# Stick-breaking attention: queries or keys on the partitions, the running sum as triangle products or as scans

## The reference

```python
def block(args):
    qblk, qi = args
    z = jnp.einsum('bhqd,bhkd->bhqk', qblk, kh).astype(jnp.float32) * scale
    strict = kidx[None, :] < qi[:, None]
    log_beta = jax.nn.log_sigmoid(z)
    log_1mb = jnp.where(strict, jax.nn.log_sigmoid(-z), 0.0)
    between = lax.cumsum(log_1mb, axis=3, reverse=True) - log_1mb
    a = jnp.exp(jnp.where(strict, log_beta + between, -jnp.inf))
    return jnp.einsum('bhqk,bhkd->bhqd', a, vh)
```

## Time and profile before

| | us |
|---|---|
| median of three runs | 2451.89 (2450.37 to 2454.68) |
| profiled execution | 2442.98 |
| its span | 2441.2 |
| TensorE busy | 2342.7 (96%) |
| VectorE busy | 1131.7 (46%) |
| ScalarE busy | 852.2 (35%) |
| GpSimd busy | 541.6 (22%) |

### The profile page before, as it was taken

One profiled execution on the slowest core, in us unless ns is written; L12 is line 12 of the kernel. 1 busy time (PEld: TensorE's weight loads), 2 busy tenths in 40 slices (PEclk: granted clock), 3 DMA queues, 4 the chain that ended last, 5 costly groups with the idle time before them and its releaser, 6 DMA issues.

```text
span 2441.2 us, 34782 instructions
## 1 busy us (share of the span) xinstructions
PE 2342.7 (96%) x14548; PEld 1771.8 (73%) x14548; DVE 1131.7 (46%) x1498; ACT 852.2 (35%) x1468; POOL 541.6 (22%) x244
## 2 busy tenths in 40 slices
PE   7999999999999998999999999999999999999997
PEld 4777765555578775878888888888767677778875
DVE  6776745446566244352112122122434656477554
ACT  4444455556535222142022122022333522354321
POOL 2321212111120221321212222222222122213221
PEclk9999999999999998999999999999999999999999
DMA  3211101103023010111111111112221001100022
GB/s 135 72 46 50 52 26 35 52 26 121 27 79 129 26 35 10 51 37 50 52 43 52 43 52 43 52 43 70 83 75 44 18 27 43 37 27 12 4 105 78
DMA packets 37276, 126.03 MB, mean 52 GB/s; under 512 B 3856, under 2 KB 4368, under 8 KB 36752
## 3 DMA queue, kind: packets, MB, share of 16 engines
q1 hardware_dynamic: 30864, 103.30, 13.7%
q10 hardware_dynamic: 6272, 20.69, 2.2%
HBM read 114.53 MB, written 8.91 MB: 51 GB/s over the span
## 4 chain that ended last, share of the span: by engine, by line
PE 87%; DVE 7%; ACT 4%; issue 1%; DMA 0%; ACTq 0%; DVEq 0%
PE PS L186 22%; PE PS L188 21%; PE PS L187 21%; PE PS L902 2%; PE PS L1906 2%; PE PS L887 2%; PE PS L739 1%; PE PS L762 1%; PE PS L1144 1%; PE PS L914 1%; PE PS L1121 1%; PE PS L927 1%; PE PS L320 1%; PE PS L1527 1%; DVE arena L401 1%
## 5 line engine op out<-in xcount | busy, mean ns | idle before, releaser
L186 PE MATMUL PS<-u_r,w_hi 128*128 128x512 f32 x1280 | 520.4, 407 | 8.7 <-DVE arena_r L196 3.5
L188 PE MATMUL PS<-u_r,w_lo 128*128 128x512 f32 x1280 | 505.6, 395 | 0.0
L196 POOL TENSOR_TENSOR w_lo<-w_raw,w_hi 128x1024 fp32r<-128x1024 f32 x143 | 360.8, 2523 | 587.6 <-ACT w_hi L192 581.6
L187 PE MATMUL PS<-arena_r,w_hi 128*128 128x512 f32 (+1 forms) x1152 | 439.3, 381 | 0.0
L235 POOL TENSOR_TENSOR w_hi<-w_raw,const 128x1024 fp32r<-128x1024 f32 x77 | 151.1, 1962 | 1202.3 <-PE PS L186 1050.9
L186 PEld LDWEIGHTS PS<-u_r,w_hi 128*128 128x128 f32 x1280 | 240.6, 188 | 87.9 <-issue 16.0
L188 PEld LDWEIGHTS PS<-u_r,w_lo 128*128 128x128 f32 x1280 | 240.8, 188 | 57.0
L187 PEld LDWEIGHTS PS<-arena_r,w_hi 128*128 128x128 f32 x1152 | 217.0, 188 | 43.2 <-issue 0.7
L186 PE MATMUL PS<-h_r,w_hi 128*128 128x512 f32 x512 | 210.5, 411 | 4.3 <-DVE u_r L409 4.0
L188 PE MATMUL PS<-h_r,w_lo 128*128 128x512 f32 x512 | 202.9, 396 | 0.0
L187 PE MATMUL PS<-y_r,w_hi 128*128 128x512 f32 x512 | 201.0, 393 | 0.0
(11 more groups left out here) (395 smaller groups left out, 3547.9 us busy)
## 6 DMA issues: line engine op xcount, KB each, us to landing
w_raw<-in_w SPq DMA_DIRECT2D x174, 512.0 KB, 3.6
arena<-in_w SPq DMA_DIRECT2D x10, 512.0 KB, 5.2
h<-in_xT ACTq DMA_DIRECT2D x1, 4096.0 KB, 14.3
u<-parked_stream ACTq DMA_DIRECT2D x1, 4096.0 KB, 13.0
out<-arena SPq DMA_DIRECT2D x16, 256.0 KB, 2.0
parked_stream<-h ACTq DMA_DIRECT2D x6, 512.0 KB, 2.7
h<-in_xT SPq DMA_DIRECT2D x8, 256.0 KB, 7.4
h<-in_xT ACTq DMA_DIRECT2D x8, 256.0 KB, 9.2
```

Of the source, the lines that this page charges most:

```text
L186: first = pe.matmul(out, a[0], b[0], start=start, stop=False)
L187: pe.matmul(out, a[0], b[1], start=False, stop=False)
L188: return first, pe.matmul(out, a[1], b[0], start=False, stop=stop)
L196: return e.tensor_tensor(out, x, hi_part.bitcast(F), ALU.subtract)
```

## The change

Queries stand on the partitions and keys along the columns. An item is now one block of 128 queries against up to four key blocks, the nearest keys first; a unit still has 12 items and the same number of blocks. Their sizes in order are 1, 2, 3, 4, 1, 4, 2, 4, 3, 4, 4, 4.

- The running sum over keys is a scan along the columns, from right to left, on VectorE: one for each head, its two inputs max(z, 0) and the log, its start the sum left by the item before. The triangle products, the column totals, the decay, the 0/1 mask and the accumulation of the output on VectorE are gone.
- ScalarE writes max(z, 0) with a Relu from the score banks. VectorE then subtracts the sums from the scores.
- The weights need keys on the partitions for the value product: TensorE transposes the exponents block by block into bank 6, in one round (both heads, up to two blocks) or two (one head each), and ScalarE's Exp takes each round out.
- The value products accumulate in bank 7 over all key blocks of four query blocks; ScalarE copies them out twice a unit. They are one block pair of 128 columns at a time.
- The mask product is made with the scores.
- Chunks of q, k, v are made in two halves of 12 products (`part`), spread over the items. The "w" chunks stand one item later, the last one behind the last item.
- Transposes and weights run two items behind the scores, values three.
- Three constants (384 columns) are no longer loaded. One of the two weight tiles lies in `pos_f`, free at that time.

The core of the diff:

```diff
+        SB_PARTS = {j: {s: [(c, s % 2)] for s in range(12) for c in [("qkv"[s // 4], N_DA + j + 1, s // 2 % 2)]} for j in range(2)}
+        SB_PARTS[2] = {s: [(("qkv"[n // 4], UNITS - 1, n // 2 % 2), n % 2) for n in ns]
+                       for s, ns in enumerate(((0, 1), (2, 3), (4,), (5,), (6, 7), (8,), (9,), (10,), (11,)))}
...
-        SB_ITEMS = [(kb, half) for kb in range(4) for half in range(2)] + [(kb, 1) for kb in range(4, NT)]
+        SB_ITEMS = [(t, lo) for t in range(NT) for lo in (range(0, t + 1, 4))[::-1]]
...
+        def sb_scores(pe, g):
+            w, s = N_DA + g // SB_N, g % SB_N
+            t, lo, n, cols = sb_item(g)
+            if g >= 2:
+                pe.wait_ge(S("sb_e"), g - 1)
...
+                m = pe.matmul(bank(2 + 2 * (g % 2) + hd)[:, :cols], q[r, t * P:(t + 1) * P], k[r, lo * P:lo * P + cols],
+                              start=True, stop=not diag)
...
+        def sb_turn(pe, g, rd):
+            t, lo, n, cols = sb_item(g)
+            pe.wait_ge(S("sb_e"), g + 1)
+            if sb_turned(g, rd) > 1:
+                pe.wait_ge(S("sb_a"), sb_turned(g, rd) - 1)
...
+            for x, hd in enumerate(hds):
+                for b in range(n):
+                    m = pe.transpose(bank(6)[:, (x * n + b) * P:(x * n + b + 1) * P], Eb[:, g % 2, hd, b * P:(b + 1) * P], cst("ident"))
+            m.then_inc(S("sb_turned"), 1)
+
+        def sb_values(pe, g):
...
+            for b in range(n):
+                for hd in range(2):
+                    m = pe.matmul(PS[64 * hd:64 * hd + 64, 7 * HALF + t % 4 * P:7 * HALF + (t % 4 + 1) * P],
+                                  values_of(w)[1][:, lo + b, 64 * hd:64 * hd + 64], AT[g % 2][:, hd, b * P:(b + 1) * P],
+                                  start=first and b == 0, stop=last and b == n - 1)
+            m.then_inc(S("sb_av"), 1)
 
         def sb_pe(pe, g):
             if g < SB_ALL:
...
+                sb_scores(pe, g)
+            if g < 2:
+                da_values(pe, DA_N - 2 + g)
+            if 2 <= g < SB_ALL + 2:
+                sb_turn(pe, g - 2, 0)
+            if g < SB_ALL:
+                for c, part in sb_parts(*divmod(g, SB_N)):
+                    chunk_pe(pe, c, part)
+            elif g == SB_ALL:
+                chunk_pe(pe, CHUNK_ORDER[-1])
...
+            if 3 <= g < SB_ALL + 3:
+                sb_values(pe, g - 3)
+            if 2 <= g < SB_ALL + 2 and len(sb_rounds(g - 2)) > 1:
+                sb_turn(pe, g - 2, 1)
...
         def sb_act(act, g):
             if g < SB_ALL:
                 act.wait_ge(S("sb_z"), g + 1)
                 if g >= 2:
-                    act.wait_ge(S("sb_sp"), g - 1)
+                    act.wait_ge(S("sb_sums"), g - 1)
                 act.activation(sb_cols(ab, g), sb_z(g), ACT.Abs).then_inc(S("sb_abs"), 1)
+            if 2 <= g < SB_ALL + 2:
+                sb_weights(act, g - 2, 0)
+            if g < SB_ALL:
                 act.wait_ge(S("sb_abs"), g + 1)
                 act.activation(sb_cols(ab, g), sb_cols(ab, g), ACT.Exp, scale=-1.0).then_inc(S("sb_exp"), 1)
+                if g >= 2:
+                    act.wait_ge(S("sb_sums"), g)
+                    act.wait_ge(S("sb_e"), g - 1)
+                act.activation(sb_cols(sp, g), sb_z(g), ACT.Relu).then_inc(S("sb_relu"), 1)
                 act.wait_ge(S("sb_exp"), g + 1)
                 act.activation(sb_cols(ab, g), sb_cols(ab, g), ACT.Ln, bias=1.0).then_inc(S("sb_ln"), 1)
...
             if g < SB_ALL:
-                for c in sb_chunks(g // SB_N, g % SB_N):
+                for c in sb_chunks(*divmod(g, SB_N)):
                     chunk_act(act, c)
+            if 3 <= g < SB_ALL + 3:
+                sb_take_o(act, g - 3)
+            if 2 <= g < SB_ALL + 2 and len(sb_rounds(g - 2)) > 1:
+                sb_weights(act, g - 2, 1)
...
         def sb_dve(dve, g):
             if g < SB_ALL:
                 j, s = divmod(g, SB_N)
+                t, lo, n, cols = sb_item(g)
                 dve.wait_ge(S("sb_ln"), g + 1)
+                dve.wait_ge(S("sb_relu"), g + 1)
+                whole = lo + n == t + 1
+                for hd in range(2):
+                    sums = sp[:, g % 2, hd, :cols][:, ::-1]
+                    m = dve.tensor_tensor_scan(sums, sums, ab[:, g % 2, hd, :cols][:, ::-1],
+                                               0.0 if whole else sp[:, (g - 1) % 2, hd, 0:1], ALU.add, ALU.add)
+                m.then_inc(S("sb_sums"), 1)
+                dve.wait_ge(S("sb_sums"), g + 1)
                 if g >= 2:
...
+                    dve.wait_ge(S("sb_turned"), sb_turned(g - 2, len(sb_rounds(g - 2)) - 1))
+                dve.tensor_tensor(sb_cols(Eb, g), sb_z(g), sb_cols(sp, g), ALU.subtract).then_inc(S("sb_e"), 1)
```

More of the change, by code:

```diff
@@ L414, in in_, with chunk_product @@
             return lambda k, lo, hi: t[:, k, lo:hi]
-        def chunk_product(pe, g, b, x, h, width=T, ready=None, order=range(KC), free=None, inner=None, at=0):
+        def chunk_product(pe, g, b, x, h, width=T, ready=None, order=range(KC), free=None, inner=None, at=0, part=None):
             w = min(width, HALF)
             for k in order:
+                if part is not None and k // (KC // 2) != part:
+                    continue
                 if k == order[3] and inner is not None:
@@ L642, in chunk_pe @@
                 g = 3 * w + UNIT_PANEL[what]
-                if h == 0:
+                if h == 0 and part != 1:
                     panel_in(pe, g)
@@ L650, in ready @@
                         wait_split(pe, "mix", h)(k)
-                m = chunk_product(pe, g, b, u_mix, h, ready=ready, free=(h == 1) if w == 0 and what == "k" else None)
-            m.then_inc(S("proj_mm"), 1)
+                m = chunk_product(pe, g, b, u_mix, h, ready=ready, free=(h == 1) if w == 0 and what == "k" else None, part=part)
+            if part != 0:
+                m.then_inc(S("proj_mm"), 1)
         def chunk_act(act, c):
@@ L856, in sb_item, with sb_rounds @@
+        AT = [t.rearrange("p (h k) -> p h k", h=2) for t in (ar.take(T), pos_f)]
         def sb_item(g):
-            kb, half = SB_ITEMS[g % SB_N]
-            lo = max(kb * P, half * HALF)
-            return kb, lo, (half + 1) * HALF, kb // 4 == half
+            t, lo = SB_ITEMS[g % SB_N]
+            n = min(t + 1 - lo, 4)
+            return t, lo, n, n * P
         SB_ALL = (UNITS - N_DA) * SB_N
-        SB_CARRY = [g for g in range(SB_ALL) if sb_item(g)[0] > 0]
-        SB_DIAG = [g for g in range(SB_ALL) if sb_item(g)[3]]
+        def sb_rounds(g):
+            n = sb_item(g)[2]
+            return [(0, 1)] if n <= 2 else [(0,), (1,)]
@@ L866, in sb_z, with sb_turned @@
+        def sb_turned(g, rd):
+            return sum(len(sb_rounds(x)) for x in range(g)) + rd + 1
         def sb_z(g):
-            kb, lo, hi, diag = sb_item(g)
-            return bank(2 + 2 * (g % 2), 2).rearrange("p (h q) -> p h q", h=2)[:, :, :hi - lo]
+            return bank(2 + 2 * (g % 2), 2).rearrange("p (h k) -> p h k", h=2)[:, :, :sb_item(g)[3]]
         def sb_cols(t, g):
-            kb, lo, hi, diag = sb_item(g)
-            return t[:, g % 2, :, :hi - lo]
+            return t[:, g % 2, :, :sb_item(g)[3]]
@@ L2570, in _ @@
             dve.wait_ge(S("const_late"), 16)
[L2571 removed]
+            for g in range(SB_ALL + 1):
                 sb_dve(dve, g)
[L2573 to L2574 removed]
             y1_dve(dve, KC)
@@ L2791, in _ @@
                 da_act(act, g)
-            for g in range(SB_ALL + 1):
+            for g in range(SB_ALL + 3):
                 if g == SB_ALL - SB_N - 3:
@@ L2973, in _ @@
                 da_pe(pe, g)
-            for g in range(SB_ALL + 1):
+            for g in range(SB_ALL + 2):
                 sb_pe(pe, g)
```

198 lines of the change are left out of this document (74 added, 124 removed).

## The result

The changed kernel takes 2410.68 us (median, 2409.01 to 2415.41), the kernel before on the same chip 2451.3: a ratio of 0.9835, interval 0.9818 to 0.9852, so 40.6 us less, where 27 less had been forecast. A second run of both on another occasion gave 2410.77 and 2449.58, ratio 0.984 (0.9826 to 0.9853).

What follows compares the result with a forecast made beforehand. TensorE's work was taken to bound the stick-breaking stage. Its units summed to 308.5 us against 340.1 (-32); charging 4 for VectorE beside GpSimd and 1 for the clock left -27 from the median 2451.89: 2425 us, range 2401 to 2446.

Steps and rivals of the forecast that it cites:

- TensorE's terms: Stick-breaking stage: triangle products -66, column totals -26, values +8, transposes +32; net -52 us, the most that can be won.
- the longer of both engines at each item: Stage: neither TensorE nor ScalarE runs a step ahead, so each step takes the longer; middle unit 66, with additions 73.
- ScalarE's price: Stage: Relu 39 and other terms priced by instruction durations; ScalarE rises by about 30 us to 230.
- The fourth unit: Last unit of the stage: longer ones 64, with additions 70, then a 7.5 tail; 77.5 us against 81.6.
- The 4 us charged for VectorE's place: Stage: scans and GpSimd operations lock each other out in SBUF; 4 us charged, with 0 and 57 as ends.
- the additions of 3, 1 and 3: Middle unit: 3 us for ways between engines, 1 for instruction gaps, 3 that the same arithmetic missed before.
- the rival of the doubled scan: Stage: a scan pair takes 4.8 us, breaking the cover in 24 four-block items; +21, 2473; within a 0.08 chance.
- my own case: Whole kernel: 15 to 42 us faster, 2410 to 2437 us, chance 0.60.
- the case of TensorE alone: Stage: ScalarE's longer steps overlap shorter neighbours, only TensorE counts; -45 to -52, 2400 to 2407; chance 0.12.
- Doubled hand-overs: Stage: exchanges between engines cost about twice as much; only -7 to -13, 2439 to 2445; chance 0.14.
- VectorE as the bound: Stage: the scan pair waits out GpSimd (+28, 2480) or runs longer backwards; slower; chance 0.08.
- table loads: Stage: Relu needs two loads of 1.283 us for each of 48 items on ScalarE; +33, 2485; chance 0.01.

Runs made afterwards that it cites:

- Experiment 1: Changed kernel with each ScalarE instruction of a step made to wait for the one before it; 2434.92 us, 0.9961 of the kernel before.
- experiment 2: Two edits of the changed kernel: max(z, 0) left out, the scan taking the log twice, 0.9804; the maximum on VectorE instead of ScalarE, 0.9843.
- the second trace: Another trace of the unaltered changed kernel; its stage takes 305.9 us, where the first trace has 301.9.
- experiment 5: Changed kernel, seam of third and fourth unit: unneeded products added 0.9854; new values' transposes apart 0.9841; both 0.9831; transposes apart and seam rearranged 0.9814, with added products 0.9817.
- experiment 3: Changed kernel with the scan replaced by a plain addition of the same inputs, the running sum left out; 0.9798 of the kernel before.
- experiment 4: Changed kernel with whole q, k, v chunks at their old items, 0.9924; kernel before with only the halves spread over the items, 0.9988.

## Why the prediction was right in direction and too small

- **TensorE's terms.** Net 52 us to win at most; its busy time in the stage fell by 44.7. In the middle unit, at a granted clock of 1.00 on both sides, it fell by 12.9 us (80.15 to 67.23), a quarter of 52. The transposes' group has 288 records with 49.3 us busy, less 0.17 for each of 80 rounds 36, where 32 was priced. The price of the middle unit, 63, plus the 3 us that the same arithmetic had missed before, is 66; TensorE is busy 67.2 there. This held.
- **The step that failed: the longer of both engines at each item.** Over TensorE's 66 the prediction put 7 us for ScalarE's longer steps, gaps and hand-overs in the middle unit; 3.2 us of idle time were there (70.4 less 67.2), of it 1.4 at item 0 (the evacuation) and 1.25 at item 4 (the scan beside GpSimd), so next to nothing was left for ScalarE's longer steps. The mis-sized term is ScalarE's price: durations, 230 us, where the starts follow 0.10 to 0.12 us closer, 211 us. Experiment 1 gives ScalarE that price back, and somewhat more, and the middle unit goes to 78.7; experiment 2 takes Relu away, and the steps said to be bound by ScalarE don't move. By units: 72.2, 70.4 and 76.9 against 76, 73 and 82, in all 11.5 us better (8.5 by the second trace).
- **The fourth unit.** 77.5 predicted, 82.4 measured. VectorE's crowd at the seam had been priced as two longer ScalarE steps (7.0, 6.8) in the third unit and nothing in the fourth, whose items 0 and 1 took 7.4 and 7.3 us, though item 0 has no piece of the projection. Of the 7.3 some 1.6 are the clock's (experiment 5), for which the prediction had put 1 us and said that TensorE had slack; it had slack at the seam and none behind it. The 4 us charged for VectorE's place are there in size: 3.2 us in front of item 5 of three units, the rest at this seam.
- **Sum.** Stage 308.5 + 5 charged, against 301.9: 11.6 us less; 27 became 38.2 in the stage. By the second trace, 305.9, it is 7.6 less and 34.2. The sum has a slip: the additions of 3, 1 and 3 are 7, as in the middle unit, but by the figures given the third and fourth unit got 6; with 7 the stage would be 310.5 and the gain 25. In the rival of the doubled scan 4.8 less 2.8 is 2.0, not 2.2, so 2468 and not 2473. Of the signs named, TensorE's busy time (281), the scans at 1.2 and the waits of the transposes came; ScalarE near 230 did not, and the unit least improved is the fourth, not the third.
- **The scans.** 1.2 us for 512 columns, backwards and in place, is right (the median of all 96 is 1.199); the mean of the 512-column ones is 1.447, because GpSimd's operations hold some up to 3.0. The mechanism was right, and it is small on the path: 9 to 10 us for the whole scan length (experiment 3), seam included.
- **The rivals.** The result, 2410.7, lies at the very edge of my own case (2410 to 2437), 14 us from its figure and 4 from the case of TensorE alone (2400 to 2407); that case's reason, that ScalarE's longer steps are absorbed, is what was found. That the wide range held it is no merit of the sum. Doubled hand-overs, VectorE as the bound, table loads: none; the profile has no load in the stage and Relu costs Abs's price.
- **Where the gain comes from** was left open by the sum, and experiment 4 answers it: neither the formulation nor the spread has it. Of the middle unit's 13.3 us the formulation alone has 4.7 and the spread alone 2.7; the other 5.9 are only there with both. The shares are rough, since the transposes of new values stand elsewhere in the two runs than in the kernels that they are set against.

## What to carry to other kernels

Price an engine by the distance from start to start of its instructions in the order that they will have, not by their durations: the same six instructions cost ScalarE 0.2 us each less when none follows the one it waits for. When work is taken off the bounding engine, lay what is left of it evenly beside the other engines' longest items in the same edit; without that, half of this gain was not there (21 of 40 us), in the middle unit partly as idle time and partly as a lower clock. And look at the seams, where queues written for other purposes pile up behind one another, apart from the steady steps: in the unit behind the seam this change gained nothing. What a low clock costs is read behind the idle stretch, at the first step in which the engine is busy without a gap, and not in the stretch itself.

## What the runs showed of the hardware

- ScalarE, 128 x 1024 float32: 1.03 to 1.06 us long, 0.91 to 0.95 from start to start when the next doesn't wait for it, 1.09 to 1.17 when it does; 512 columns: 0.60 long, 0.47 and 0.69.
- A scan of two SBUF inputs beside GpSimd's splitting is held up to 3.03 us instead of 1.2, and GpSimd's operation took 3.15 for 2.5 in the same place. The Trainium skill (SBUF — State Buffer, Who interferes with whom) says that the later of two such operations waits for the other; the trace agrees, for both engines. Here it cost TensorE 1.25 us at one item in each of the first two units and 0.69 in the fourth.
- Max from PSUM in float32: 1.22 us for 1024 columns on VectorE against 1.03 for Relu on ScalarE; the 48 of all sizes 45.6 against 39.1 us.
- TensorE's granted clock went to 0.54 to 0.76 behind a stretch in which it had been busy 3 to 4.3 of 6 us. Where TensorE waited this cost nothing; at the next step that it filled, the same work took 5.68 us at 1.00, 7.25 at 0.76 and 8.43 at 0.65. Added products kept the clock at 1.00, and the medians could not tell it from no change.
